# The first blocks multiplied before the norm is known, and scaled while they leave PSUM

## The reference

```
h    = x * rsqrt(mean(x*x over 1024) + eps) * norm1_w        # one factor per token
proj = h @ w_in[0]                                           # 1024 -> q, k, v (1024 each), z, b, a, ...
qkv  = silu(depthwise_conv(concat(q, k, v), 5 taps))         # centred, along the tokens
q, k = l2norm per head of 128
beta = sigmoid(b);  g = -exp(A_log) * softplus(a + dt_bias)  # 16 rows each: 8 heads, 2 directions
```

## Time and profile before

| | us |
|---|---|
| runs | 2712.94 (median), 2712.76, 2715.92 |
| profiled execution, its own time | 2710.24 |
| its span | 2708.5 |
| mean granted TensorE clock | 0.988 |
| TensorE matmul busy | 2593.3 (96%) |
| VectorE busy | 1446.2 (53%) |
| ScalarE busy | 989.6 (37%) |
| GpSimd busy | 1093.0 (40%) |

### The profile page before, as it was taken

The page is one execution under the profiler, slowest core; times in us unless marked ns, Lnnn a source line. Parts: engine busy times, 40 slices in busy tenths (PEclk is TensorE's granted clock), DMA queues, the critical chain, the costliest instruction groups (busy, mean ns, idle before and its releaser), DMA issues.

```text
span 2708.5 us, 47436 instructions
## 1 busy us (share of the span) xinstructions
PE 2593.3 (96%) x17631; PEld 2256.8 (83%) x17631; DVE 1446.2 (53%) x2090; ACT 989.6 (37%) x1811; POOL 1093.0 (40%) x560
## 2 busy tenths in 40 slices
PE   6999899899999999999898999999999999999999
PEld 5987888878987788887877689999999976788887
DVE  7874767515247642426787547345467234645533
ACT  5655434132222422224243753221243366422222
POOL 4335343244444444445435124444444311444443
PEclk9999999999999999999998999999999999999999
DMA  3223010132222222223211012222222200223222
GB/s 103 79 79 93 13 14 13 38 127 86 93 88 90 96 95 98 93 93 101 71 40 47 2 37 89 87 92 90 89 94 79 79 25 2 93 90 96 93 93 101
DMA packets 88948, 201.82 MB, mean 75 GB/s; under 512 B 36292, under 2 KB 38390, under 8 KB 88800
## 3 DMA queue, kind: packets, MB, share of 16 engines
q1 hardware_dynamic: 82812, 192.19, 22.2%
q10 hardware_dynamic: 5988, 7.58, 0.8%
HBM read 193.81 MB, written 5.92 MB: 74 GB/s over the span
## 4 chain that ended last, share of the span: by engine, by line
issue 46%; PE 29%; POOL 11%; DVE 7%; POOLq 3%; ACT 3%; DVEq 1%; ACTq 0%; SPq 0%; DMA 0%
PE ps L553 20%; POOL wl L517 10%; PE ps L1314 5%; POOLq L2460 2%; DVE work L2363 1%; DVE top L2360 1%; PE ps L1431 1%; PE ps L1430 1%; POOL xbl L2469 1%; PE ps L2123 1%; ACT dec L1573 0%; ACT dec L1566 0%; POOLq L2468 0%; DVE xbh L700 0%; POOLq L130 0%
## 5 line engine op out<-in xcount | busy, mean ns | idle before, releaser
L517 POOL TENSOR_TENSOR wl<-wraw,wh 128x1024 fp32r<-128x1024 f32 x352 | 879.5, 2499 | 1181.4 <-ACT wh L509 1181.4
L509 ACT ACTIVATE wh<-wraw 128x1024 fp32r<-128x1024 f32 x352 | 371.4, 1055 | 517.6 <-PE ps L553 500.3
L553 PE MATMUL ps<-xah,wh 128*128 128x264 f32 (+1 forms) x2656 | 496.6, 328 | 20.3 <-ACT xah L758 7.7
L553 PE MATMUL ps<-xah,wl 128*128 128x264 f32 (+1 forms) x2656 | 487.6, 324 | 0.0
L553 PE MATMUL ps<-xal,wh 128*128 128x264 f32 (+1 forms) x2656 | 485.1, 323 | 0.2 <-DVE xal L745 0.2
L553 PEld LDWEIGHTS ps<-xah,wh 128*128 128x128 f32 x2656 | 403.5, 190 | 75.8 <-issue 21.1
L553 PEld LDWEIGHTS ps<-xah,wl 128*128 128x128 f32 x2656 | 401.9, 189 | 41.0 <-issue 1.0
L553 PEld LDWEIGHTS ps<-xal,wh 128*128 128x128 f32 x2656 | 400.5, 188 | 41.1 <-DVE xal L745 0.5
L707 DVE TENSOR_TENSOR res<-res,stage 128x512 f32 (+3 forms) x112 | 80.4, 718 | 409.9 <-ACT stage L625 409.9
L553 PE MATMUL ps<-xbh,wh 128*128 128x264 f32 (+1 forms) x1392 | 276.7, 337 | 6.5 <-DVE xbl L702 3.6
L553 PE MATMUL ps<-xbl,wh 128*128 128x264 f32 (+1 forms) x1392 | 272.9, 334 | 0.0
(11 more groups left out here) (384 smaller groups left out, 2967.5 us busy)
## 6 DMA issues: line engine op xcount, KB each, us to landing
wraw<-in_w SPq DMA_DIRECT2D x352, 512.0 KB, 3.3
res<-in_x SPq DMA_DIRECT2D x4, 528.0 KB, 5.8
z_out<-stage ACTq DMA_DIRECT2D x8, 256.0 KB, 2.1
z_again<-z_out ACTq DMA_DIRECT2D x1, 2048.0 KB, 9.4
res<-in_x ACTq DMA_DIRECT2D x1, 2048.0 KB, 15.1
out<-res SPq DMA_DIRECT2D x8, 256.0 KB, 4.2
block_out<-yy SPq DMA_DIRECT2D x18, 56.0 KB
block_in<-mt SPq DMA_DIRECT2D x60, 8.0 KB
```

What stands on the lines that cost most here:

```text
L509: act.activation(wh[:, s * DM:(s + 1) * DM], wraw[:, s * DM:(s + 1) * DM], ACT.Copy).then_inc(hi_done, 1)
L517: pool.tensor_tensor(wl[:, s * DM:(s + 1) * DM], wraw[:, s * DM:(s + 1) * DM], wh[:, s * DM:(s + 1) * DM].bitcast(F32), ALU.subtract).then ...
L553: mm = pe.matmul(ps[:, to + h, 0:width], ws[:, s * DM + kk * P:s * DM + (kk + 1) * P], x[:, x0:x0 + width], start=(h not in [o[0] for o in ...
```

## The change

The norm's factor belongs to a token, so it can be multiplied in after the product over the model width. Block 0 and the blocks of j = 0 to 8 (UNSCALED = 9) are now made from x * gain without `rstd`, in new tiles `xuh` (high parts, ScalarE) and `xul` (low parts, VectorE), and VectorE multiplies by `rstd` when a block leaves PSUM (`leave(j)` writes `cpad`; `dve_ba` for block 0). These blocks go round three pairs of banks (6, 2, 0). ScalarE's `taps` then has two copies in place of three, from SBUF. From j = 9 on the blocks use `xah` and `xal` as before. The tiles `scaled` are made one by one in a ring of four: two by VectorE ahead of the first convolution, then one behind each `conv(j)` for j = 0 to 5; ScalarE rounds tile j-1 at the end of its step j, and GpSimd subtracts it behind the weight block of step j, for j = 1 to 8.

The sum of squares is no longer added on VectorE: TensorE multiplies each squared tile by the ones (16 calls in place of 2), GpSimd makes two of the squares, ScalarE six. The constants are loaded by SyncE behind x and the first two weight blocks, not by ScalarE. The decay's last five pieces move from j = 0 to 4 to j = 2, 4, 6, 8, 10; its transposes on TensorE from j = 7 to 12, its sums from j = 9 to 14, ScalarE's parts from j = 8 and 10 to 13 and 15, VectorE's from j = 10 to 15. The clearing of buffers that share memory with `xuh` and `xul` goes behind `conv(9)`.

```diff
+SCALED = 4
+UNSCALED = 9
...
+    FIRST_OPS = [("hi", 0), ("hi", 1), ("hi", 2), ("square", 2), ("hi", 3), ("square", 3), ("weights", 0), ("hi", 4),
+                 ("square", 4), ("hi", 5), ("square", 5), ("hi", 6), ("hi", 7), ("square", 6), ("square", 7)]
...
+        pe.wait_ge(hi_done, 1)
+        for m in range(KT):
+            pe.wait_ge(nfirst, FIRST_COUNT["hi", m])
+            both_halves(wh, xuh, m, start=(m == 0))
+            if m > 1:
+                sums(m - 2)
+        pe.wait_ge(lo_done, 1)
+        for m in range(KT):
+            both_halves(wl, xuh, m)
+        sums(KT - 2)
+        sums(KT - 1).then_inc(nsum, 1)
...
+        for m in range(KT):
+            pe.wait_ge(nscaled, m + 1)
+            mm = both_halves(wh, xul, m, stop=(m == KT - 1))
+        mm.then_inc(block_done, 1)
...
+    def dve_scale(dve, m):
+        if m >= SCALED:
+            dve.wait_ge(nlo, m - SCALED + 3)
+        dve.scalar_tensor_tensor(scaled[m % SCALED][:, :], tile_at(res, m), gains[:, m:m + 1], rstd[:, :], ALU.mult,
+                                 ALU.mult).then_inc(nscaled, 1)
+
+    def act_scaled_hi(act, m):
+        act.wait_ge(nscaled, KT + m + 1)
+        act.activation(tile_at(xah, m), scaled[m % SCALED][:, :], ACT.Copy).then_inc(nhi, 1)
+
+    def pool_scaled_low(pool, m):
+        pool.wait_ge(nhi, m + 1)
+        pool.tensor_tensor(tile_at(xal, m), scaled[m % SCALED][:, :], tile_at(xah, m).bitcast(F32), ALU.subtract
+                           ).then_inc(nlo, 1)
...
         for j in range(24):
-            products(pe, Blk(QKV + j, 0), xah, xal, KT)
+            b = QKV + j
+            if j < UNSCALED:
+                products(pe, Blk(b, 0), xuh, xul, KT, at=first_bank(b), free=b - 2)
+            else:
+                products(pe, Blk(b, 0), xah, xal, KT, fresh=0 if j == UNSCALED else None)
...
-            if j == 7:
+            if j == 12:
                 pe_prep_turn(pe)
-            if j == 9:
+            if j == 14:
                 pe_prep_sums(pe)
...
+            if j < UNSCALED:
+                act.wait_ge(acc_free, num(b) + 1)
+                act.wait_ge(conv_done, j + 1)
+                x = cpad[u][:, 2:2 + T]
+                act.activation(cmid[u][:, :], x, ACT.Copy, scale=convw[:, j * 5 + 2:j * 5 + 3])
+                act.activation(ctap[u][:, 2:2 + T], x, ACT.Copy, scale=convw[:, j * 5:j * 5 + 1]).then_inc(taps_done, 1)
+                return
...
+            if 1 <= j <= KT:
+                act_scaled_hi(act, j - 1)
...
+        def leave(j):
+            b = QKV + j
+            dve.drain()
+            dve.wait_ge(block_done, b + 1)
+            wait(dve, conv_done, j)
+            dve.tensor_tensor(two(cpad[j % 2][:, 2:2 + T]), pair_of(first_bank(b)), two(rstd[:, :]), ALU.mult
+                              ).then_inc(acc_free, 1)
+
         decay = dve_decay(dve)
+        dve_scale(dve, 0)
+        dve_scale(dve, 1)
         next(decay)
+        leave(0)
         next(decay)
...
         for j in range(24):
+            if j + 1 < UNSCALED:
+                leave(j + 1)
             conv(j)
-            if j < 5:
+            if j + 2 < KT:
+                dve_scale(dve, j + 2)
+            if j in (2, 4, 6, 8, 10):
                 next(decay)
-            if j == 6:
+            if j == UNSCALED:
+                buffers_of_the_first()
+            if j == KT + 2:
+                dve.wait_ge(nhi, KT)
                 dve.memset(uu[:, :], 0.0).then_inc(d_y, 1)
-            if j == 10:
+            if j == 15:
                 dve_prep_sums(dve)
...
     def act_ba(act):
 
-        split_hi(act, Blk(1, 0))
-        act.wait_ge(block_done, 1)
-        act.activation(two(beta[:, 0:T]), acc(Blk(0, 0), 16), ACT.Sigmoid)
-        act.activation(two(gdec[:, 0:T]), ps[32:48, 0:2, 0:HT], ACT.Copy).then_inc(acc_free, 1)
-        act.drain()
+        act.wait_ge(acc_free, 1)
+        act.activation(beta[:, 0:T], beta[:, 0:T], ACT.Sigmoid)
         act.activation(gdec[:, 0:T], gdec[:, 0:T], ACT.Identity, bias=rowvec[:, 0:1]).then_inc(prep_act, 1)
...
     def pe_prep_turn(pe):
+        pe.wait_ge(acc_free, QKV + UNSCALED)
         pe.wait_ge(prep_dve, 1)
```

More of the change, by code:

```diff
@@ L352, in build_program @@
     norm_sq = [place(f"norm_sq{m}", [P, T], F32, b_at + m * F) for m in range(KT)]
-    scaled = [place(f"scaled{m}", [P, T], F32, b_at + (KT + m) * F) for m in range(KT)]
+    scaled = [place(f"scaled{i}", [P, T], F32, d_at + 4 * 4 * (T + 8) + i * F) for i in range(SCALED)]
+    assert d_at + 4 * 4 * (T + 8) + SCALED * F <= nc.sbuf_usable_end
+    xuh = place("xuh", [P, KT * T], F32R, phase_at + 16 * TS * 4)
+    xul = place("xul", [P, KT * T], F32R, oacc_at)
     rq = region(phase_at + 17 * F)
@@ L708, in add_residual @@
         return post
[L712 to L715, removed]
+    POOL_SQUARES = (0, 1)
+    FIRST_OPS = [("hi", 0), ("hi", 1), ("hi", 2), ("square", 2), ("hi", 3), ("square", 3), ("weights", 0), ("hi", 4),
+                 ("square", 4), ("hi", 5), ("square", 5), ("hi", 6), ("hi", 7), ("square", 6), ("square", 7)]
+    FIRST_COUNT = {op: n + 1 for n, op in enumerate(o for o in FIRST_OPS if o[0] != "weights")}
@@ new lines, in pe_first, with both_halves, sums @@
+    def pe_first(pe):
+        def both_halves(ws, x, kk, start=False, stop=False):
+            for h in range(2):
+                at = kk * T + h * HT
+                mm = pe.matmul(ps[:, first_bank(0) + h, 0:HT], ws[:, kk * P:(kk + 1) * P], x[:, at:at + HT],
+                               start=start, stop=stop)
+            return mm
+        def sums(m):
+            if m in POOL_SQUARES:
+                pe.wait_ge(nsq_pool, POOL_SQUARES.index(m) + 1)
+            else:
+                pe.wait_ge(nfirst, FIRST_COUNT["square", m])
+            for h in range(2):
+                mm = pe.matmul(ps[:, 4 + h, 0:HT], ones[:, :], norm_sq[m][:, h * HT:(h + 1) * HT], start=(m == 0),
+                               stop=(m == KT - 1))
+            return mm
+        pe.wait_ge(hi_done, 1)
[9 more added lines that the diff above has]
+        sums(KT - 1).then_inc(nsum, 1)
@@ L724, in act_norm, with pool_first @@
         norms["act"] += 1
-        split_hi(act, Blk(0, 0))
+        split_hi(act, Blk(1, 0))
         act.wait_ge(nsum, norms["act"])
         act.activation(two(rstd[:, :]), pair_of(4), ACT.Sqrt, bias=eps[:, 0:1], scale=1.0 / DM).then_inc(nroot, 1)
[L729 to L733, removed]
+    def pool_first(pool):
+        for m in POOL_SQUARES:
+            pool.wait_ge(x_in[m // 2], 16)
+            pool.tensor_tensor(norm_sq[m][:, :], tile_at(res, m), tile_at(res, m), ALU.mult).then_inc(nsq_pool, 1)
@@ L739, in dve_norm, with tile_of, first_bank @@
         dve.drain()
[L741 to L762, removed]
+    def dve_scale(dve, m):
[10 more added lines that the diff above has]
+                           ).then_inc(nlo, 1)
+    def tile_of(buf, m):
+        return buf[:, m * T:(m + 1) * T]
+    def first_bank(b):
+        return (6, 2, 0)[b % 3]
     def gain_at(gi, m):
@@ L1030, in dve_qkv, with buffers_of_the_first @@
             dve.memset(ctap[u][:, 0:2], 0.0)
-        dve.memset(qkv[:, :].rearrange("p (k t) -> p k t", t=TS)[:, :, T:TS], 0.0)
+        dve.memset(qkv[:, 0:16 * TS].rearrange("p (k t) -> p k t", t=TS)[:, :, T:TS], 0.0)
         dve.memset(hroot[0:48, :], 1.0)
[L1033 to L1038, removed]
+        def buffers_of_the_first():
+            dve.wait_ge(block_done, QKV + UNSCALED)
+            dve.memset(qkv[:, 16 * TS:24 * TS].rearrange("p (k t) -> p k t", t=TS)[:, :, T:TS], 0.0)
+            for g in range(2):
+                dve.memset(hinvr[g][32:64, :].bitcast(F32), 0.0)
+            dve.memset(pick[:, :].bitcast(F32), 0.0)
+            dve.drain()
+            for at in range(0, 112, 32):
+                dve.tensor_copy(pick[at:at + 4, at // 32 % 2:8:2], ident[0:4, 0:4])
+        def leave(j):
+            b = QKV + j
+            dve.drain()
+            dve.wait_ge(block_done, b + 1)
+            wait(dve, conv_done, j)
+            dve.tensor_tensor(two(cpad[j % 2][:, 2:2 + T]), pair_of(first_bank(b)), two(rstd[:, :]), ALU.mult
+                              ).then_inc(acc_free, 1)
         decay = dve_decay(dve)
+        dve_scale(dve, 0)
+        dve_scale(dve, 1)
         next(decay)
+        leave(0)
         next(decay)
@@ L1044, in conv @@
             u = j % 2
-            dve.wait_ge(acc_free, QKV + j + 1)
+            if j < UNSCALED:
+                dve.wait_ge(taps_done, j + 1)
+            else:
+                dve.wait_ge(acc_free, QKV + j + 1)
             o = cout[u][:, :]
@@ L3086, in _ @@
             pool.sem_inc(nlo, 2)
+            pool_first(pool)
             split_lo(pool, Blk(0, 0))
-            pool_norm_apply(pool)
+            split_lo(pool, Blk(1, 0))
             loaded(pool)
-            split_lo(pool, Blk(1, 0))
-            pool_segment(pool, "qkv")
+            for j in range(24):
+                split_lo(pool, Blk(QKV + j + 1, 0))
```

(2 more changed lines are left out.)

70 lines of the change are left out of this document (47 added, 23 removed).

## The result

The changed kernel is slower: 2737.31 us (median of four runs, 2730.87 to 2738.37) against 2712.85 (four runs), a ratio of 1.0086 [1.0073, 1.0098]. The forecast was 2724.0 with a range to 2732: the sign was right, and the size (11.3 us) a little under half of what was measured (24.5). The profiled execution of the changed kernel took 2737.77, its span 2735.5.

The account below looks back on a forecast made before the run. A serial chain bounds the head, then TensorE and VectorE are both full. Head 6.7 us earlier, conv(9) 8.0 late, apply(0) 12.8 late, 1.5 given back: 11.3 slower, 2721.5, plus 2.7 for the median: 2724, range 2706 to 2732.

Parts of the forecast that it names:

- The head: Start up to conv(0): the serial chain to the norm factor gets shorter, conv(0) at 43.8, 6.7 us earlier.
- the slow pace lasts or the constants come late: Rival in the head: norm at 39 instead of 29, 10 us more, 2734; chance 0.05.
- VectorE's queue: conv(0) to conv(9): VectorE is full, added work lengthens it one for one; conv(9) ends at 117.4, 8.0 late.
- TensorE's wait at j=12: Behind block j=12, ahead of the transposes: TensorE stalls 5 us until VectorE's last decay piece is ready at 127.1.
- a head start that outlives the stage: Rival: VectorE's multiplications hide in its waits, TensorE stays the bound up to j=16; faster, 2704 to 2710; chance 0.23.
- a cancelling: Rival: gains and losses cancel, low parts cost 0, within 0.2% of before, 2713; chance 0.10.
- the low parts: GpSimd's eight subtractions beside VectorE up to conv(9): each delays VectorE 0.9, 7.2 us in all, bounds 0 to 9.6.
- The leaves: VectorE's products of PSUM and rstd: leave(2) to leave(8) add 7 x 0.75 = 5.3 us after conv(0) starts.
- rival (1): Behind conv(9) VectorE's 11 us of idle time take the delay: 5 us slower, 2718; chance 0.12.
- 12.8 late, all handed on to block j=18: First multiplication of a q block by its norm, apply(0), at 169.5 against 156.7, delays TensorE's block j=18 in full.
- 1.5 given back: The block after j=18 recovers 1.5 us, since before it had waited for apply(1); net 11.3 slower.

Follow-up runs that it names:

- e5: e2 with GpSimd's eight low parts of the scaled tiles replaced by clearing the same tiles, so they read nothing; 2717.07 us, ratio 1.0020.
- e9: e2 with each of the nine products on leaving PSUM made twice on VectorE; 2729.63 us, ratio 1.0058.
- e2: The changed kernel with the whole decay preparation early: pieces behind j = 0 to 4, transposes behind j=9, sums behind j=11; 2724.89 us, ratio 1.0049.
- e8: The kernel before with two more clearings on VectorE behind each of conv(0) to conv(8); 2720.44 us, ratio 1.0030.
- e3: The changed kernel with VectorE's preparation sums ahead of conv(15) instead of behind it; 2728.39 us, ratio 1.0057.
- e4: The kernel before with only the decay's pieces and preparation moved to the change's late places; 2724.12 us, ratio 1.0043.
- e10: The changed kernel with 40 useless matmuls in TensorE's wait ahead of the transposes behind j=12; 2733.30 us, ratio 1.0071.
- e1: The changed kernel with the decay's five pieces on VectorE back behind j = 0 to 4; 2735.74 us, ratio 1.0081.
- e6: e2 with the last two sums of squares ahead of block 0's 16 matmuls with the low weights; 2722.19 us, ratio 1.0036.
- e7: The kernel before with its constants issued by SyncE behind x and the first two weight blocks, not by ScalarE; 2710.87 us, ratio 0.9995.

## Why the prediction was right in sign and wrong in size

**The head held, in part by luck.** Sum of squares complete at 24.9 forecast, 24.85 measured; norm factor 29.2 and 29.04; block j=1 35.5 and 36.66; conv(0) 43.8 and 44.97. The rival that the slow pace lasts or the constants come late is refuted: no wait for a constant appears in the waits of TensorE, ScalarE or VectorE. Two terms were off and cancel: the high part of the first weights was done at 10.9 and not at 10.0, since the table load (1.28 us, from 5.02) was left out, and TensorE needed 13.9 us from there and not 14.9.

**VectorE's queue held.** From conv(0) to conv(6) a convolution every 8.0 us ((93.01 - 44.97)/6), forecast 7.8; conv(9) ended at 118.9, forecast 117.4; the decay was ready at 128.9, forecast 127.1; TensorE's wait at j=12 was 5.08, forecast 5. VectorE was busy 55.42 of 58.90, so the rival of a head start that outlives the stage is refuted, and with it a cancelling. Of the terms, the low parts (0.9 each forecast, 0.8 by e5) were right. The leaves (5.3 us for seven) may have been too dear: nine second products cost 2.4 to 3.0 in e9. That e9 was built on e2, and doubles the leaves instead of taking them away, leaves open whether the first ones are as cheap. If they are, another term was too small by as much, since the stretch from conv(0) to the end of conv(9) came out (73.9 us, forecast 73.6), and no run says which.

**The free time of VectorE.** By rival (1) it takes the delay. It takes a part: of 13.2 us at conv(9) 8.6 are left at the end in e8, of 9.2 in e2 8.1. That doesn't save the change.

**The step that failed** is the last one: "12.8 late, all handed on to block j=18, which waited for apply(0) already". I had put VectorE's preparation sums ahead of conv(16), ending at 165.3, and counted them only as a delay of apply(0). But the spreading behind j=16, which comes before block j=17, waits for these sums (`prep_dve`). Block j=17 and its head sums (7.37 + 1.02) therefore stood behind the sums instead of beside them: j=17 came 20.5 us late (149.60 to 170.10). I had read the waits that had a length before; this one had none, so no row of before shows it, and only the kernel's text does. With just that wait removed (e3) the stage delay is 12.3. That this is close to the forecast's 11.3 is partly luck: block j=15 of the changed kernel began 12.2 late (148.50 against 136.32 in TensorE's timelines), where the forecast had 7.0, and the sums, placed ahead of conv(15), ran in part in time in which VectorE was idle. e4 shows the same wait, 7.66 us, made without the rest of the change.

**A second term was missing:** TensorE's pace after a long wait. I priced the 5 us at j=12 as 5 us. Block j=13 cost 2.8 more (8.63 against 5.85), and e10 got 2.8 back by keeping TensorE busy. e1 got 2.8 too, by having no wait so long there: the wait itself was only VectorE's lag, and it turned up before the head sums instead. Block j=17 paid 1.5 more (7.37), which e3 removed with the wait.

From the forecast to the measured delay, by the starts in the two traces:

| | us |
|---|---|
| forecast | 11.3 |
| apply(0) at 172.24, not at 169.5, since TensorE was later at j=15 | 2.7 |
| block j=18 at 178.75, behind block j=17; apply(0) alone would have let it start at about 173.4 | 5.4 |
| after block j=18: 2.7 more (conv(17) waited for block j=17), not 1.5 given back | 4.2 |
| measured | 23.6 |

The 173.4 is an estimate: apply(0) plus the 1.16 us that lay between apply(0) and block j=18 before. TensorE was 5.2 later at j=15 than forecast, nearly all of it explained: 2.8 for the slow block, 1.8 because the decay was ready at 128.9 and not at 127.1, and 0.4 because the transposes took 1.0 and not 0.6.

From the experiments:

| | us of stage delay |
|---|---|
| what stays with the preparation early (e2) | 8.1 |
| sums that the spreading waits for, with the slow block behind them (after less e3) | 11.2 |
| slow block j=13 (after less e10) | 2.8 |
| sum, against 23.6 measured | 22.1 |

The rows of this second table come from different kernels and need not add up (e3's has 0.6 of the slow block in it); the 1.5 that is left is within the scatter. Of the 8.1, GpSimd's low parts are 5.1 (e5) and the late sums of squares 1.7 (e6); if the parts add up, 1.3 remain for leaves and scalings beyond the head start.

## What to carry to other kernels

When work is moved down a hand-written order, list every wait that the program of the bound engine has from there on, with the place where its producer now stands, and not only the waits that have a length in the profile of before: here it was one of no length that grew to 7.7 us. An earlier start on one engine brings nothing when another is full over the same stretch, so the ledger to make is that of the fuller one. Price a new idle stretch of TensorE with the slower matmuls behind it: here 1.9 to 2.8 us after 5.1 and 1.5 after 7.7.

## What was unexpected of the hardware

- Operations added on VectorE that a running GpSimd operation doesn't lengthen absorbed more than half of their own price, since the one behind them was held up for less time: 7.0 us of products cost 2.4 to 3.0 (e9).
- A longer wait didn't mean a slower block behind it: 8.63 after an idle 5.1 us (7.75 in e3), 7.37 after 7.7, 7.66 in the block that followed 4.1 us (j=1). Behind a wait of 2.63 or 2.64 us block j=22 took 7.00 in one execution (before, first fence), 8.35 in another (e10, second) and about 5.9 in a third (e3), which is the usual pace:

```profile
188.57 7.00 PE ps L553 x48
```

```profile
208.38 8.35 PE ps L560 x48
```

- A table load on ScalarE with its next operation ready behind it cost 1.28 us, in the kernel before (6.94 to 8.24) as in e7 (4.86 to 6.15).
